# Float16 for the choice of experts, the gate tiles' dots ahead of the low parts, and sixteen dots in a head's turn in place of fifteen

## The chip, the core and the metric

The kernel runs on one core of a Trainium2 chip, as one program. The engines spoken of are TensorE (PE, with PEld for its weight loads), VectorE (DVE), ScalarE (ACT), GpSimd (POOL) and SyncE (SP, which only starts transfers here). Each follows its own list of instructions in order, and they meet through semaphores. The metric is the time of one execution on the device in microseconds. Lower is better.

## The reference

The program computes two transformer blocks one after the other, for 512 tokens of width 1024. The change lies wholly in the second half of the first block, `peer_ffn`, a feed-forward layer that picks its experts by product keys:

```
q = (xi @ w_q).reshape(n, PEER_HEADS, 2, PEER_KEY_DIM)          # 8 heads
s = jnp.einsum('nhpc,hpkc->nhpk', q, sub_keys)                  # 128 keys a side
ts, ti = lax.top_k(s, PEER_TOPK)                                # 16 a side
cand_s = ts[:, :, 0, :, None] + ts[:, :, 1, None, :]            # 16 x 16 sums
cand_i = ti[:, :, 0, :, None] * PEER_NKEYS + ti[:, :, 1, None, :]
best_s, best_p = lax.top_k(cand_s, PEER_TOPK)
idx = jnp.take_along_axis(cand_i, best_p, axis=-1)              # 16 experts a head
gate = jax.nn.softmax(best_s, axis=-1)
act = jax.nn.gelu(jnp.einsum('nd,nhkd->nhk', xi, u[idx]))
return jnp.einsum('nhk,nhkd->nd', gate * act, v[idx])
```

There are 128 x 128 = 16384 experts, with a row of 1024 numbers each in `u` and in `v`.

## The kernel before

**Two ways through the experts.** For the first 384 tokens (ND) the kernel computes the products with all 16384 experts on PE: 128 slabs of `u`, 128 experts each, give activations that are stored in DRAM ("early"), and later a gate matrix, zero where an expert was not picked, multiplies them before the slabs of `v` are applied. For the last 128 tokens (one to a partition) it does what the reference does: it fetches the 8 x 16 = 128 picked rows of `u` for each token and takes their dot products with the token. Pick k is a column of 128 row numbers in `own_at`. POOL fetches it with one indirect transfer of 128 rows (512 KB), L2435 in `own_fetch`, and DVE takes the dot product in `own_dots` at L2123, one custom instruction for each pick. There are 8 row buffers for the picks of the head stage and 4 for those of the gate tiles, and a fetch waits until its buffer's last dot is done (semaphore `own_dotted`). A dot waits for its row (`own_in`).

**The head stage.** Eight turns, one a head. PE's part of turn h: two query slabs, the scores of both sides (L1078), and ten slabs of `u` woven in (`woven`), 12 slabs in all. Each slab passes as three float16 products, so its float32 numbers are cut into a high part (ACT, L519, which also scales the slab in place, L521) and a low part (POOL, L532, `cut_low_scaled`). PE waits for the low part. POOL runs three slabs ahead of PE: its loop of turn h starts with the low part of the fourth slab of head h (woven slab number 1, counted from 0), and each of its 12 steps j is one low part and then the fetches of that step.

**Which picks POOL fetches when.** In the turns 1 to 6 POOL's loop spreads TURN_PICKS = 15 fetches over the 12 steps: turn h fetches the picks (h-1)*15 to (h-1)*15+14. A head has 16 picks, and the first pick of each head waits on POOL for `head_done`, that is for DVE's last instruction of that head's choice (L2110). The first fetch of a turn has such a wait as well. So the pick that waits stands at step 1 in turn 2, at step 2 in turn 3, at step 3 in turns 4 and 5 and at step 4 in turn 6; the fetches ahead of it are picks of a head before. Turn 7 fetches four more picks in its last steps.

**DVE's turn.** DVE starts turn h when the scores of head h are copied out of PSUM (`s_out`), and then runs `choose`. It is in three parts with a third of the dots ahead of or between them (`own(0)`, `own(1)`, `own(2)`): first the dots 0 to 4 of the turn, then the top 16 of each side (L2058 to L2063), then the dots 5 to 9, then the candidates (L2068), the top 16 of them (L2071 to L2079, with `gsub_out` given at L2076), then the dots 10 to 14, then the experts' numbers: for each side a comparison of `posf` with 0 to 15 into `sel` (L2089), a product of `sel` with `tif` (L2094) and a sum over it (L2105), and the softmax of the gates. The last instruction is L2110, which gives `head_done`. Turns 0 and 7 have no dots. ACT's turn h+1 begins with the exponential of head h's gates (L1588), which waits for L2076; only behind it in ACT's order stand the copies of the queries (L1578) and of the scores (L1584) of head h+1.

**Between the stages.** After turn 7 PE does four more slabs, then waits for `head_done` of the last head and transposes the experts' numbers and gates (L1125). ACT copies them out (L1631), DVE casts them (from L2146 on), and the gate tiles begin.

**The gate tiles.** Six tiles of 64 tokens, each in eight octets. For an octet DVE writes one-hot matrices in float16 (`one_hots`, L2159 to L2164, which gives `hot_out`), ACT writes half of the low ones (L1644, which waits for L2159), PE multiplies them into the gate matrix (L1140 and L1141, which wait for `hot_out`) and ACT copies that out (L1662). In each tile PE also does five slabs of `u`. Their high parts come from ACT (L513), their low parts from DVE (L526). DVE's order is written out in `tile_turn`: behind the octet's one-hots stand the low parts that are due (`cuts.upto`), then a dot if the octet's number is in TILE_DOTS = (0, 2, 4, 5, 6). The eight dots that are left (TAIL_PICKS) come behind the tiles.

## Time and profile before

| | |
|---|---|
| three runs | 2394.67, 2402.81, 2405.39 us |
| median | 2402.81 us |
| the profiled execution | 2406.6 us, of which the span of the trace is 2404.9 us |
| granted TensorE clock over the span | 0.988 |
| head stage, from the first query slab to the wait for the last head | 405.6 to 852.9 us |
| gate tiles | 874.5 to about 1065 us |
| value slabs, and the second block | about 1098 us to the end |

The profile was read in this order: the page (busy shares and the chain that ended last), the view of waits for the head stage, the busy time of the engines turn by turn, the time line of POOL and DVE at the start of a turn, and the same for one gate tile. Times in the time line count from the start of the span. A wait's releaser is the instruction that set the semaphore last.

### The profile page before, as it was taken

The numbers are of one execution on the slowest core, as the hardware profiler recorded it, in microseconds if no ns is written. First come the engines' busy times: TensorE is split into PE (matmuls) and PEld (weight loads), VectorE is DVE, ScalarE is ACT, GpSimd is POOL, SyncE is SP. The second block draws the span as 40 slices with busy tenths as digits, with TensorE's granted clock in tenths as the row PEclk, the third lists the DMA queues.
The fourth block names the chain that finished last, engine by engine and source line by source line (L and its number), as shares of the span: only waits on it lengthen the run. The fifth ranks groups of instructions, "written<-read, shape, count | busy, mean of one in ns | idle before, by whom it ended". The sixth has DMA issues, their size and how long they took to land.

```text
span 2404.9 us, 38222 instructions
## 1 busy us (share of the span) xinstructions
PE 2324.7 (97%) x13522; PEld 1292.8 (54%) x13522; DVE 1698.6 (71%) x2994; ACT 1104.9 (46%) x1677; POOL 553.1 (23%) x418
## 2 busy tenths in 40 slices
PE   7999999999999989999999999999999999999998
PEld 4446764555555556665555555564444444444454
DVE  5327765588899979977988888878453447776235
ACT  4266443665666668864333333343522233333133
POOL 0001001667788631123322222204000010000001
PEclk9999999999999999999999999999999999999989
DMA  5200022587889659989999999933232323233321
GB/s 180 79 27 1 1 71 88 185 275 281 309 313 332 225 172 345 343 322 359 381 364 361 362 361 357 362 126 114 88 114 97 104 89 105 96 102 108 102 74 53
DMA packets 164871, 470.67 MB, mean 196 GB/s; under 512 B 17744, under 2 KB 70736, under 8 KB 163984
## 3 DMA queue, kind: packets, MB, share of 16 engines
q1 hardware_dynamic: 109312, 289.48, 34.8%
q0 software_dynamic: 36864, 134.23, 15.1%
q10 hardware_dynamic: 18576, 45.36, 5.0%
q8 instruction: 76, 1.25, 0.2%
q14 instruction: 43, 0.35, 0.0%
HBM read 421.56 MB, written 47.45 MB: 195 GB/s over the span
## 4 chain that ended last, share of the span: by engine, by line
PE 74%; DVE 16%; ACT 2%; issue 2%; POOL 2%; DMA 2%; DVEq 2%; SPq 0%; ACTq 0%
PE psum L552 22%; PE psum L553 22%; PE psum L554 22%; DVE arena L2123 4%; DVEq L2048 2%; DMA arena<-in_urows,arena 2%; POOL arena L532 1%; PE psum L434 1%; POOL arena L2435 1%; PE psum L1140 1%; PE psum L1017 1%; PE psum L1141 1%; PE psum L895 1%; DVE arena L526 1%; DVE arena L1919 1%
## 5 line engine op out<-in xcount | busy, mean ns | idle before, releaser
L552 PE MATMUL psum<-arena 128*128 128x384 f16 (+2 forms) x3648 | 1262.4, 347 | 18.9 <-DVE arena L483 7.6
L553 PE MATMUL psum<-arena 128*128 128x384 f16 (+2 forms) x3648 | 1265.5, 347 | 0.0
L554 PE MATMUL psum<-arena 128*128 128x384 f16 (+2 forms) x3648 | 1258.6, 347 | 0.0
L552 PEld LDWEIGHTS psum<-arena 128*128 128x128 f16 x3648 | 355.0, 97 | 353.1 <-issue 37.8
L554 PEld LDWEIGHTS psum<-arena 128*128 128x128 f16 x3648 | 354.0, 97 | 324.0 <-issue 6.7
L553 PEld LDWEIGHTS psum<-arena 128*128 128x128 f16 x3648 | 354.1, 97 | 311.2 <-issue 7.1
L526 DVE SCALAR_TENSOR_TENSOR arena<-arena 128x1024 f16<-128x1024 f32 x216 | 265.5, 1233 | 287.4 <-ACT arena L513 286.1
L513 ACT ACTIVATE arena<-arena 128x1024 f16<-128x1024 f32 x216 | 226.3, 1051 | 237.5 <-PE psum L554 226.1
L1678 ACT ACTIVATE arena<-arena 128x1024 f16<-128x1024 f32 x128 | 135.3, 1057 | 299.7 <-PE psum L554 278.6
L532 POOL TENSOR_TENSOR arena<-arena 128x1024 f16<-128x1024 f32 x104 | 230.7, 2218 | 103.9 <-ACT arena L521 102.3
L445 POOL TENSOR_TENSOR arena<-arena 128x512 f32<-128x512 f32 x15 | 19.8, 1318 | 890.4 <-ACT arena L399 890.4
L2435 POOL DMA_INDIRECT arena<-in_v,arena x128 | 132.5, 1035 | 356.8 <-DVE arena L2134 324.4
L2435 POOL DMA_INDIRECT arena<-in_urows,arena x128 | 133.6, 1044 | 210.1 <-DVE arena L2123 153.4
L2123 DVE CUSTOM_DVE_ANT_0 arena<-arena,psum 128x1024 f32<-128x1024 f32 x128 | 151.4, 1215 | 29.7 <-DMA arena<-in_urows,arena 28.1
L2134 DVE SCALAR_TENSOR_TENSOR arena<-arena 128x1024 f32<-128x1024 f32 x126 | 161.0, 1279 | 1.7 <-DMA arena<-in_v,arena 1.7
L2211 DVE SCALAR_TENSOR_TENSOR arena<-arena 128x1024 f16<-128x1024 f32 x128 | 156.0, 1219 | 0.0
L1604 ACT ACTIVATE arena<-psum 128x384 f32<-128x384 f32 x128 | 62.2, 486 | 133.6 <-PE psum L554 130.8
L2205 DVE TENSOR_TENSOR arena<-arena 128x384 f16<-128x384 f32 x128 | 71.4, 558 | 61.8 <-ACT arena L1683 61.4
L519 ACT ACTIVATE arena<-arena 128x1024 f16<-128x1024 f32 x104 | 109.0, 1048 | 11.0 <-DMA arena<-in_w 10.9
L521 ACT ACTIVATE arena<-arena 128x1024 f32<-128x1024 f32 x104 | 109.9, 1057 | 3.3
L1785 ACT ACTIVATE arena<-psum 128x512 f32<-128x512 f32 x44 | 26.3, 598 | 143.6 <-PE psum L554 143.6
L399 ACT ACTIVATE arena<-arena 128x512 f32<-128x512 f32 (+1 forms) x48 | 29.7, 630 | 86.1 <-DVE arena L2030 33.4
(258 smaller groups left out, 2226.8 us busy)
## 6 DMA issues: line engine op xcount, KB each, us to landing
arena<-in_w SPq DMA_DIRECT2D x320, 512.0 KB
arena<-in_v SPq DMA_DIRECT2D x128, 512.0 KB
early_activations<-arena ACTq DMA_DIRECT2D x124, 192.0 KB
arena<-early_activations SPq DMA_DIRECT2D x124, 192.0 KB
gate_matrix<-arena ACTq DMA_DIRECT2D x5, 4096.0 KB, 16.1
arena<-gate_matrix SPq DMA_DIRECT2D x32, 640.0 KB
arena<-in_xT SPq DMA_DIRECT2D x4, 512.0 KB, 6.3
arena<-in_urows,arena POOLq DMA_INDIRECT x128
```

What stands on the lines that cost most here:

```text
L513: nc.scalar.activation(wh[:, s, :], wraw[:, s, :], ACT.Copy, scale=WS).then_inc(high_cut, 1)
L521: nc.scalar.activation(wraw[:, s, :], wraw[:, s, :], ACT.Copy, scale=WS).then_inc(high_cut, 1)
L526: nc.vector.scalar_tensor_tensor(out=wl[:, s, :], in0=wraw[:, s, :], scalar=WS, in1=wh[:, s, :], op0=ALU.mult, op1=ALU.subtract).then_inc( ...
L532: nc.gpsimd.tensor_tensor(wl[:, s, :], wraw[:, s, :], wh[:, s, :], ALU.subtract).then_inc(low_cut, 1)
L552: nc.tensor.matmul(ps, a_h, b_h, start=first, stop=False)
L553: nc.tensor.matmul(ps, a_h, b_l, start=False, stop=False)
L554: return nc.tensor.matmul(ps, a_l, b_h, start=False, stop=last)
L1678: nc.scalar.activation(vh[:, s, :], vraw[:, s, :], ACT.Copy, scale=WS).then_inc(vhigh_cut, 1)
L2123: nc.vector.tensor_tensor_reduce(out=x, in0=x, in1=own_tok, scale=1.0, scalar=0.0, op0=ALU.mult, op1=ALU.add, accum_out=own_dot[:, k:k + 1 ...
L2134: ins = nc.vector.scalar_tensor_tensor(out=to, in0=x, scalar=by, in1=to, op0=ALU.mult, op1=ALU.add)
L2211: nc.vector.scalar_tensor_tensor(out=vl[:, s, :], in0=vraw[:, s, :], scalar=WS, in1=vh[:, s, :], op0=ALU.mult, op1=ALU.subtract).then_inc( ...
L2435: nc.gpsimd.indirect_dma_start(own_row(b, k >= PICKS), None, table, bass.IndirectOffsetOnAxis(own_at[:, k % PICKS:k % PICKS + 1], 0)).then ...
```

## The change

It has four parts. The lists of instructions on PE and ACT stay as they are.

1. **Float16 in the choice.** `tif`, `posf` and `sel` become float16, in half of the words they had. A float16 copy of the numbers 0 to 15, `io16h`, is made once in turn 0. The comparison (L2089) and the product (L2094) now read and write float16. The sum (L2105) reads float16 and still writes float32. The numbers are below 128, so they stay exact.
2. **Sixteen dots in a head's turn.** TURN_PICKS goes from 15 to 16, so that the head stage holds 96 picks in place of 90. The parts of a turn have 5, 5 and 6 dots. POOL's spread of the fetches over its steps follows: one, one, two, and so on four times over.
3. **Four dots in a gate tile.** TILE_DOTS loses octet 5, so that the tiles hold 24 dots in place of 30.
4. **The tiles' dots ahead of the low parts.** In `tile_turn` the dot of an octet stands right behind its one-hots, ahead of the low parts that are due.

```
-TURN_PICKS = 15
+TURN_PICKS = 16
-TILE_DOTS = (0, 2, 4, 5, 6)
+TILE_DOTS = (0, 2, 4, 6)
...
-        tif = v3(r.take(2 * TT * TOP), 2)
+        tif = v3(r.take(2 * TT * TOP)[:, 0:TT * TOP].bitcast(f16), 2)
...
-        posf = v3(r.take(2 * TT * TOP), 2)
-        sel = v3(r.take(2 * TT * 256), 2)
+        posf_words = r.take(2 * TT * TOP)
+        posf = v3(posf_words[:, 0:TT * TOP].bitcast(f16), 2)
+        io16h = posf_words[:, TT * TOP:TT * TOP + TOP // 2].bitcast(f16)
+        sel = v3(r.take(2 * TT * 256)[:, 0:TT * 256].bitcast(f16), 2)
...
                         sel4(side), tiles(posf[:, side, :]).unsqueeze(3).to_broadcast(full),
-                        io16.unsqueeze(1).unsqueeze(1).to_broadcast(full), ALU.is_equal)
+                        io16h.unsqueeze(1).unsqueeze(1).to_broadcast(full), ALU.is_equal)
...
-                third = TURN_PICKS // 3
+                at_part = [part * TURN_PICKS // 3 for part in range(4)]
                 dve.wait_ge(s_out, 2 * h + 2)
+                if h == 0:
+                    nc.vector.tensor_copy(io16h, io16)
...
                     one_hots(t * OCT + i)
+                    if i in TILE_DOTS:
+                        own_dots(picks + TILE_DOTS.index(i), 1)
                     if t == 0 and i == 1:
                         dve.wait_ge(low_cut, cuts.n)
                     if i:
                         cuts.upto(N_U + e + (i - 1 + (i - 1) // 4 + ((i - 1) % 4 == 3)) // 2 + 3)
                     elif t:
                         cuts.upto(N_U + e - 1 + 3)
-                    if i in TILE_DOTS:
-                        own_dots(picks + TILE_DOTS.index(i), 1)
```

How this moves instructions is shown at two places. The rows are those of the programs' lists; what stands in brackets are the semaphores that an instruction waits for. Nearly everything lies in one tensor, `arena`, so a transfer of rows is told by `in_urows`.

The first place is POOL at the start of turn 3: the last two steps of turn 2 and the steps that follow. The low part of a slab is the TENSOR_TENSOR, a fetch is the DMA. Before:

```order
L532 TENSOR_TENSOR arena<-arena 128x1024 [waits high_cut]
L2435 DMA arena<-in_urows,arena 128x1024 [waits own_dotted] x2
L532 TENSOR_TENSOR arena<-arena 128x1024 [waits high_cut]
L2435 DMA arena<-in_urows,arena 128x1024 [waits own_dotted,head_done]
L532 TENSOR_TENSOR arena<-arena 128x1024 [waits high_cut]
L2435 DMA arena<-in_urows,arena 128x1024 [waits own_dotted]
L532 TENSOR_TENSOR arena<-arena 128x1024 [waits high_cut]
L2435 DMA arena<-in_urows,arena 128x1024 [waits own_dotted,head_done]
L532 TENSOR_TENSOR arena<-arena 128x1024 [waits high_cut]
L2435 DMA arena<-in_urows,arena 128x1024 [waits own_dotted] x2
```

In the changed program (L534 is the low part there, L2440 the fetch):

```order
L534 TENSOR_TENSOR arena<-arena 128x1024 [waits high_cut]
L2440 DMA arena<-in_urows,arena 128x1024 [waits own_dotted] x2
L534 TENSOR_TENSOR arena<-arena 128x1024 [waits high_cut]
L2440 DMA arena<-in_urows,arena 128x1024 [waits own_dotted,head_done]
L534 TENSOR_TENSOR arena<-arena 128x1024 [waits high_cut]
L2440 DMA arena<-in_urows,arena 128x1024 [waits own_dotted]
L534 TENSOR_TENSOR arena<-arena 128x1024 [waits high_cut]
L2440 DMA arena<-in_urows,arena 128x1024 [waits own_dotted] x2
L534 TENSOR_TENSOR arena<-arena 128x1024 [waits high_cut]
```

The wait for `head_done` that names the head just chosen stood in front of the third fetch of the turn (the one in front of the first asks for a head that was done long before). Now it stands in front of the first fetch, and there is no second one in the turn. The low part that stood between them, and the two fetches, are behind the wait now. The doubled fetch has moved up to the third step.

The second place is DVE in a gate tile, from the last one-hots of octet 4 to the first of octet 6. L526 is a low part of a slab, the two L2123 are one dot. Before:

```order
L2164 TENSOR_TENSOR arena<-arena 128x512
L526 SCALAR_TENSOR_TENSOR arena<-arena 128x1024 [waits high_cut]
L2123 ISA arena<-arena,psum 128x1024 [waits own_in1,own_turned]
L2123 ISA arena 128x1
L2159 TENSOR_TENSOR arena<-arena 128x1024 [waits g_done]
L2160 TENSOR_TENSOR arena<-arena 128x1024
L2162 TENSOR_TENSOR arena<-arena 128x1024 [waits hot_slab_out]
L2164 TENSOR_TENSOR arena<-arena 128x512
L2123 ISA arena<-arena,psum 128x1024 [waits own_in2,own_turned]
L2123 ISA arena 128x1
L2159 TENSOR_TENSOR arena<-arena 128x1024 [waits g_done]
```

In the changed program (L2169 ends an octet, L2125 is the dot, L528 the low part, L2164 begins an octet):

```order
L2169 TENSOR_TENSOR arena<-arena 128x512
L2125 ISA arena<-arena,psum 128x1024 [waits own_in2,own_turned]
L2125 ISA arena 128x1
L528 SCALAR_TENSOR_TENSOR arena<-arena 128x1024 [waits high_cut]
L2164 TENSOR_TENSOR arena<-arena 128x1024 [waits g_done]
L2165 TENSOR_TENSOR arena<-arena 128x1024
L2167 TENSOR_TENSOR arena<-arena 128x1024 [waits hot_slab_out]
L2169 TENSOR_TENSOR arena<-arena 128x512
L2164 TENSOR_TENSOR arena<-arena 128x1024 [waits g_done]
```

The dot of octet 4 has moved in front of the low part, and the dot of octet 5 is gone.

## Rows read from the trace of the kernel before

**Rows 1.** The page: busy time, share of the span and instructions of each engine.
```profile
PE 2324.7 (97%) x13522; PEld 1292.8 (54%) x13522; DVE 1698.6 (71%) x2994; ACT 1104.9 (46%) x1677; POOL 553.1 (23%) x418
```

**Rows 2.** Waits from 405 to 853 us: who waited for whom; us in total, times, longest.
```profile
POOL arena L2435 <- DVE arena L2110: 36.0, 6, 10.4
ACT arena L1588 <- DVE arena L2076: 30.3, 5, 8.7
DVE arena L2140 <- ACT arena L1584: 26.1, 2, 14.3
DVE arena L2123 <- DMA arena<-in_urows,arena: 24.2, 15, 3.5
...
PE psum L552 <- POOL arena L532: 4.5, 4, 2.2
PE psum L1125 <- DVE arena L2110: 4.5, 1, 4.5
```

**Rows 3.** Busy time of the engines in DVE's turns 2, 2 to 6, 6, 7.
```profile
core 0: us, PE busy (x) PEld busy (x) DVE busy (x) ACT busy (x) POOL busy (x), PEclk, DMA share, GB/s
532.70:594.00 61.30, 57.62 (x332) 32.65 (x331) 48.92 (x145) 36.77 (x45) 43.97 (x29) 0.97 0.79 284
532.70:814.10 281.40, 272.34 (x1592) 156.13 (x1591) 254.36 (x720) 176.29 (x215) 217.44 (x139) 0.99 0.84 295
758.40:814.10 55.70, 54.24 (x323) 31.31 (x321) 54.41 (x143) 35.08 (x44) 40.98 (x24) 1.00 0.76 262
814.20:852.60 38.40, 34.24 (x211) 20.10 (x209) 37.22 (x114) 24.76 (x30) 26.91 (x13) 0.98 0.72 234
```

**Rows 4.** DVE's waits for rows: turn 2 (532.7 to 594.0 us), then turn 4 (651.5 to 704.7).
```profile
DVE arena L2123 <- DMA arena<-in_urows,arena: 10.8, 5, 3.5
...
DVE arena L2123 <- DMA arena<-in_urows,arena: 1.7, 2, 1.2
```

**Rows 5.** Time line of POOL at the start of turn 3: start us, us, line, what; idle before it.
```profile
594.40 0.95 POOL L2435 DMA_INDIRECT arena<-in_urows,arena  x1 [9.04 <-DVE arena L2110]
...
597.69 0.95 POOL L2435 DMA_INDIRECT arena<-in_urows,arena  x1 [0.16 <-issue]
598.94 0.94 POOL L2435 DMA_INDIRECT arena<-in_urows,arena  x1 [0.30 <-issue]
```

**Rows 6.** Time line of DVE at the start of turn 3: the first four dots.
```profile
594.11 1.21 DVE L2123 CUSTOM_DVE_ANT_0 arena<-arena,psum 128x1024 f32<-128x1024 f32 x1
...
595.25 1.22 DVE L2123 CUSTOM_DVE_ANT_0 arena<-arena,psum 128x1024 f32<-128x1024 f32 x1
...
598.79 1.22 DVE L2123 CUSTOM_DVE_ANT_0 arena<-arena,psum 128x1024 f32<-128x1024 f32 x1 [2.33 <-DMA arena<-in_urows,arena]
...
603.56 1.22 DVE L2123 CUSTOM_DVE_ANT_0 arena<-arena,psum 128x1024 f32<-128x1024 f32 x1 [3.53 <-DMA arena<-in_urows,arena]
```

**Rows 7.** Time line of ACT around PE's wait in turn 4: activations of three woven slabs.
```profile
650.06 0.49 ACT L1604 ACTIVATE arena<-psum 128x384 f32<-128x384 f32 x1 [1.38 <-PE psum L554]
...
653.97 0.49 ACT L1604 ACTIVATE arena<-psum 128x384 f32<-128x384 f32 x1 [1.38 <-PE psum L554]
...
661.88 0.49 ACT L1604 ACTIVATE arena<-psum 128x384 f32<-128x384 f32 x1 [5.39 <-PE psum L554]
```

**Rows 8.** DVE's float32 and float16 products of two tensors: ns min/median/max over the program.
```profile
L2094 DVE TENSOR_TENSOR arena<-arena x16: 1219/1227/3166, 452.6 to 845.0; 128x1024 f32<-128x1024 f32 x16
L2089 DVE TENSOR_TENSOR arena<-arena x16: 1218/1226/3168, 450.2 to 840.8; 128x1024 f32<-128x1024 f32 x16
L2159 DVE TENSOR_TENSOR arena<-arena x48: 681/685/2519, 859.0 to 1051.5; 128x1024 f16<-128x1024 f16 x48
```

**Rows 9.** PE's waits in the gate tiles, 874 to 1062 us, then one tile's busy times.
```profile
PE psum L1140 <- DVE arena L2164: 10.2, 18, 1.1
...
920.90:951.30 30.40, 28.22 (x248) 18.99 (x248) 28.63 (x48) 25.87 (x59) 5.73 (x5) 1.00 0.92 345
```

**Rows 10.** Time line of DVE in a gate tile: the low part behind octet 4.
```profile
950.12 1.23 DVE L526 SCALAR_TENSOR_TENSOR arena<-arena 128x1024 f16<-128x1024 f32 x1 [1.62 <-ACT arena L513]
```

More of the change, by code:

```diff
@@ L2137, in _ @@
             for h in range(PH):
-                third = TURN_PICKS // 3
+                at_part = [part * TURN_PICKS // 3 for part in range(4)]
                 dve.wait_ge(s_out, 2 * h + 2)
+                if h == 0:
+                    nc.vector.tensor_copy(io16h, io16)
                 nc.vector.tensor_copy(gsum[:, 12 + h % 2:13 + h % 2], s_[h % 2][:, 0, 0:1])
-                choose(h, s_[h % 2], lambda part: own_dots((h - 1) * TURN_PICKS + part * third, third)
+                choose(h, s_[h % 2], lambda part: own_dots((h - 1) * TURN_PICKS + at_part[part],
+                                                           at_part[part + 1] - at_part[part])
                        if 0 < h < PH - 1 else None)
```

## The prediction

> **What bounds the kernel now.** The page comes first: PE is busy 97% of the span [rows 1], so only what makes PE stand or slows its clock can be won. The windows of the stages show two places with such gaps that the change touches, the head stage and the gate tiles. In the head stage the view of waits says who sets the pace [rows 2]. ACT waits 30.3 us in 5 turns for L2076 of the head before, and ACT is what hands PE its next scores. POOL waits 36.0 us for `head_done` (L2110) and so PE 4.5 us for low parts, and PE waits 4.5 us more for the last head. DVE waits for rows (24.2 us) and, only at the starts of turns 0 and 1, for scores (26.1 us in two waits). So from turn 1 on DVE's chain sets the end of the stage: five turns, 2 to 6, take 281.4 us, and turn 7, without dots, 38.4 [rows 3]. The start of turn 3 shows why early turns are longer (turn 2: 61.3 us, turn 6: 55.7 [rows 3]). DVE's first dot starts at 594.11 and the second 1.14 us later, with rows fetched ahead [rows 6]. POOL stood 9.04 us for L2110 and issues the next fetch at 594.40 [rows 5], some 0.35 us behind `head_done`. Its dot can start at 598.79, 4.4 us later; the next fetch, at 597.69, has its dot at 603.56, 5.9 us later [rows 6]. Two fetches with a low part between them stand 3.3 us apart, two in a row 1.25 [rows 5]. Row waits are 10.8 us in turn 2, where one row was fetched ahead, 1.7 in turn 4, where three were [rows 4], and none in turn 6 with five. **What spares DVE the waits is the picks of an older head at the start of a turn.**
>
> **Float16.** A float32 product L2094 takes 1.227 us, a float16 one with its inner numbers side by side 0.685 [rows 8]. Both inputs of L2094 run over 16 neighbours, so I take 0.685: 2 x 0.54 = 1.09 us a turn. The comparison L2089 has the same 1.226 us [rows 8], but one of its inputs is a single number read 16 times. Its bounds are 1.226 and 0.685, and I take the first, the row of the same pattern; the other would give 1.09 us a turn more. The float16 sum L2105 has no row: between nothing and 0.5 us each; I take nothing. For the casts I count no gain either. The copy `io16h` lies in turn 0, ahead of a wait of 11.8 us (26.1 less the longest, 14.3 [rows 2]), and costs nothing.
> The Trainium skill (Vector Engine (DVE) Microarchitecture Reference, 5.1 Performance modes) says that a two-source operation on 2-byte numbers whose input is one element read 16 times ran at the plain rate, and at the doubled rate where a row is read again. By that rule the comparison gains nothing and the product does, as taken above; no row of this trace shows it.
>
> **Sixteen dots a turn.** A dot occupies DVE for 1.14 us, so with float16 the work of a turn stays: +1.14 - 1.09. But 16 is the number of picks of a head. Turn h now fetches exactly the picks of the head just chosen, and POOL meets its wait in front of the first fetch in every turn 2 to 6. DVE asks for five of these rows at once. From `head_done` the fetches start at +0.35, +3.6, +6.9, +8.2 and +11.4 us (steps of 3.3, 3.3, 1.25 and 3.3 [rows 5]; the second to fourth low parts are ready, since ACT is up to four slabs ahead while PE stands). With 4.4 us for the first and 5.9 for the others [rows 5, 6] the dots start at 4.7, 9.5, 12.8, 14.1 and 17.3 and end at 18.5, where five dots need 5.7. That is 12.8 us of waits, 2.0 more than turn 2 has now [rows 4]. The dots of the second part come after the top 16 of both sides; their rows are then there. Bounds: rows that land the moment they are issued leave 7.9 us (POOL's pace alone); a second step of 1.5 us in landing, as from 4.4 to 5.9, for the last one gives 14.3.
> A turn is then 61.3 + 2.0 + 1.14 - 1.09 = 63.35 us. I start from turn 2 and not from turn 6, because DVE is busy 48.9 us in the one and 54.4 in the other [rows 3] with the same instructions: products and casts of DVE wait where POOL is at a low part (L2089 up to 3.168 us in place of 1.226 [rows 8]), and in turn 2 POOL stands, as it will.
> The Trainium skill (SBUF — State Buffer, SBUF: two separate sides) has it that the port pair of these two engines is held by one of them for a whole instruction; the trace agrees, with 1.94 us of surplus on L2089.
>
> **Who is last at the end of the stage.** In turn 1 the doubled fetch moves up a step, which brings one of its rows some 2 to 3.3 us sooner; of that I take 1.5 us (between 0 and 3.3). So turn 2 starts at 531.2 and turn 6 at 531.2 + 4 x 63.35 = 784.6. PE is now held at woven slab 2 in each turn, as POOL's low part for it stands behind the wait: it goes on 3.5 us after `head_done` (0.35 + 0.95 + 2.2). A woven slab takes 3.91 us (650.06 to 653.97 [rows 7]); where PE stood for 2.2 us [rows 2] the next activation came 7.91 us later [rows 7], so about 1.8 us went on a lower clock (0.97 granted in turn 2, that is stretches at 1.2 in place of 2.4 GHz [rows 3]). For a stand of 7 us I take 3. From there to the end of the stage PE has 22 woven slabs (86.0), two query slabs of 512 columns (2 x 3.91 x 512/384 = 10.4) and the scores (2): 98.4. PE arrives at 784.6 + 3.5 + 3 + 98.4 = 889.5. DVE ends turn 7 at 784.6 + 63.35 + 38.4 - 1.1 = 885.3. PE is last, and the transposes start at 889.5 in place of 852.9: **+36.6 us**. The wait of 4.5 us there [rows 2] goes, and is inside this sum. PE does not hold DVE in the turns: the next scores are copied out at 3.5 + 3 + 31.3 + 10.4 + 7 = 55 us of a turn of 63.
>
> **The gate tiles.** PE waits 10.2 us for one-hots, in 18 waits, three a tile [rows 9]. Before octet 5 DVE waits 1.62 us for ACT with the low part, with a dot behind it [rows 10]. The dot now lies in that hole (1.14 us), and the dot of octet 5 is gone (1.14 more for octets 6 and 7). Each of the three waits is at most 1.1, so all go: **-10.2 us**, at most 6 x (30.4 - 28.2) = 13 by PE's busy time in a tile [rows 9], and nothing if ACT, busy 25.9 of 30.4, becomes late instead. The low parts come 1.14 us later, but DVE makes them three slabs (over 10 us) ahead. The picks 120 to 127 stay behind the tiles as they were, and the value slabs and the second block have the same instructions.
>
> **Sum.** 36.6 - 10.2 = +26 us. On the profiled execution's 2406.6 us that is 2433; it lies 3.8 above the median of 2402.8, so I forecast 2402.8 + 26 = **2429 us**.
>
> **Rivals.**
> *Cheap rows (no change).* While POOL stands, no weights are loaded either, so rows may land at once. Then a turn waits 7.9 us, not 12.8; with comparisons at 0.685 too it is 57.4 us, turn 6 starts at 760.8, PE arrives at 865.7: +12.8 - 10.2, so 2405. For it: the transfers are the busiest resource beside PE (0.84 [rows 3]). Against it: the first row, fetched after 9 us of standing, still took 4.4 us.
> *PE sets the turn (faster).* If the rows cost under 4 us a turn, DVE falls back on `s_out`, and row waits hide behind it as in turn 1. The turn is then PE's: 3.5 + 31.3 + 10.4 + 7 = 52.2 without loss of clock. Turn 6 starts at 740.0, PE arrives at 841.9: -11 - 10.2, so 2382. It decides from row waits of about 3 us a turn downwards; the break-even is at 6. Against it stand POOL's steps of 3.3 us, which alone make 7.9.
> *PE late as well (slower still).* Loaded queues (7.4 us a row) and a longer stretch at 1.2 GHz behind each stand give turns of 66: +47, and with no gain in the tiles (ACT late) 2440 to 2450.
> *Float16 brings nothing* (L2094 stays at 1.23): 1.09 x 4 = +4 us, inside the forecast's own range.
>
> **How the numbers follow.** The forecast's mechanism, with turns of 61.5 to 65 us and 8 to 13 us won in the tiles, gives 2419 to 2439 and has 0.68. Cheap rows 0.12, PE sets the turn 0.06, PE late too 0.14. About 0.5% (12 us) is what a measurement of this kernel tells from no change. So slower by more than that 0.82, within it 0.12, faster 0.06. The range of 8 in 10 runs from 2407, at the edge of the cheap rows, to 2446.
>
> **What would show it.** Right: POOL waits for L2110's successor about 13 us in each turn 2 to 6, in front of the first fetch; five turns of 61 to 65 us; the first dot of each 4 to 5 us behind `head_done`; row waits of over 60 us in all; PE standing 6 us or more at woven slab 2; L2094 at 0.69 and L2089 at 1.23 us; no wait for `head_done` at the transposes; PE's waits for one-hots under 2 us. Wrong: turns below 58 us, or gate tiles as long as before.

## The result, and the profile after

The changed kernel takes 2425.11 us (median of seven runs) against 2403.07 us for the kernel before on the same chip (median of seven). One of the seven, 3022.67 us at a granted clock of 0.749, is a slow run that the ratio leaves out; the other six have a median of 2423.69. The ratio is 1.0092, with a 95% interval from 1.0068 to 1.0117: **slower by 22 us** (20.6 by the medians without that run), where 26 were forecast. The profiled execution took 2427.66 us, its span 2425.9 us (2404.9 before), so the spans differ by 21.0 us.

The page's busy line, beside [rows 1], shows DVE busy 26 us less and TensorE's work as before:

```profile
PE 2331.6 (96%) x13522; PEld 1299.2 (54%) x13522; DVE 1672.3 (69%) x2995; ACT 1104.1 (46%) x1677; POOL 552.4 (23%) x418
```

The view of waits from 408 to 885 us (who waited for whom: us in total, times, longest), beside [rows 2]:

```profile
ACT arena L1606 <- PE psum L556: 143.5, 77, 11.5
...
POOL arena L2440 <- DVE arena L2112: 70.1, 6, 14.1
DVE arena L2125 <- DMA arena<-in_urows,arena: 66.8, 24, 4.8
...
PE psum L554 <- POOL arena L534: 33.3, 5, 7.5
...
ACT arena L1590 <- DVE arena L2078: 11.3, 2, 8.0
```

POOL's wait for `head_done` has doubled (36.0 to 70.1 us), DVE's for rows has nearly tripled (24.2 to 66.8), and PE now stands 33.3 us for low parts where it stood 4.5. ACT's wait for L2078 (L2076 before), which had been the sign that DVE's chain sets the pace, has shrunk from 30.3 to 11.3 us: ACT now stands in front of its activations (L1606, 143.5 us), behind a late PE, and so comes late to L1590 itself. Two chains are held by the same wait, DVE's by its rows and PE's by its low parts.

The windows of turns 2 to 6, turn 2, turn 6, turn 7 and of the stretch from the transposes to the first octet, beside [rows 3] (columns as there):

```profile
535.40:847.10 311.70, 277.21 (x1577) 157.51 (x1578) 238.02 (x732) 174.56 (x212) 220.79 (x145) 0.93 0.78 276
535.40:596.20 60.80, 53.44 (x304) 30.41 (x304) 46.63 (x148) 35.28 (x43) 41.90 (x28) 0.94 0.78 278
779.20:847.10 67.90, 62.09 (x361) 35.67 (x362) 52.09 (x147) 37.67 (x46) 53.24 (x33) 0.95 0.80 280
847.20:879.70 32.50, 32.50 (x202) 19.28 (x201) 30.95 (x115) 23.84 (x29) 22.11 (x12) 1.00 0.76 243
884.70:903.70 19.00, 17.13 (x110) 10.52 (x109) 13.76 (x15) 13.33 (x21) 11.76 (x6) 1.00 0.54 176
```

Turns 2 to 6 take 311.7 us in place of 281.4. The turns start at 535.4, 596.3, 657.4, 718.3, 779.1 and 847.2: four of 60.8 to 61.2 us and one, turn 6, of 68.

The start of turn 2 shows how. First POOL's time line (start us, us, engine, line, what; in brackets the idle time before it and who ended it), then DVE's:

```profile
535.76 0.95 POOL L2440 DMA_INDIRECT arena<-in_urows,arena  x1 [13.76 <-DVE arena L2112]
536.73 2.15 POOL L534 TENSOR_TENSOR arena<-arena 128x1024 f16<-128x1024 f32 x1
539.03 0.95 POOL L2440 DMA_INDIRECT arena<-in_urows,arena  x1 [0.16 <-issue]
...
542.31 0.95 POOL L2440 DMA_INDIRECT arena<-in_urows,arena  x1 [0.16 <-issue]
543.57 0.94 POOL L2440 DMA_INDIRECT arena<-in_urows,arena  x1 [0.30 <-issue]
...
546.85 0.96 POOL L2440 DMA_INDIRECT arena<-in_urows,arena  x1 [0.16 <-issue]
```
```profile
540.11 1.22 DVE L2125 CUSTOM_DVE_ANT_0 arena<-arena,psum 128x1024 f32<-128x1024 f32 x1 [4.56 <-DMA arena<-in_urows,arena]
...
543.98 1.22 DVE L2125 CUSTOM_DVE_ANT_0 arena<-arena,psum 128x1024 f32<-128x1024 f32 x1 [2.64 <-DMA arena<-in_urows,arena]
...
548.01 1.22 DVE L2125 CUSTOM_DVE_ANT_0 arena<-arena,psum 128x1024 f32<-128x1024 f32 x1 [2.80 <-DMA arena<-in_urows,arena]
...
549.26 1.22 DVE L2125 CUSTOM_DVE_ANT_0 arena<-arena,psum 128x1024 f32<-128x1024 f32 x1
...
553.19 1.22 DVE L2125 CUSTOM_DVE_ANT_0 arena<-arena,psum 128x1024 f32<-128x1024 f32 x1 [2.70 <-DMA arena<-in_urows,arena]
```

`head_done` comes at 535.5, the end of L2112. The five fetches start on POOL 0.3, 3.5, 6.8, 8.1 and 11.4 us behind it, one low part of 2.15 us between most of them, and the dots start 4.35, 4.95, 5.70, 5.69 and 6.34 us behind their fetches (the fourth dot follows the third without a row wait, so its row may have been there sooner). Of the 18.9 us from `head_done` to the end of the fifth dot, 12.7 are waits. Over a whole turn DVE stands 12.8 to 14.3 us in front of dots, in each of the turns 2 to 6.

PE at the same moment (matmuls of 384 columns):

```profile
539.02 0.48 PE L554 MATMUL psum<-arena 128*128 128x384 f16 x1 [4.70 <-POOL arena L534]
539.29 0.53 PE L555 MATMUL psum<-arena 128*128 128x384 f16 x1
...
543.13 0.39 PE L555 MATMUL psum<-arena 128*128 128x384 f16 x1
```

PE has stood 4.70 us for the low part that POOL began at 536.73. It comes back with matmuls of 0.53 us that start 0.32 us apart, and keeps that pace until 543.1; then they take 0.33 us again and start 0.16 us apart. The granted clock is 0.50 from 539.0 to 543.1 and 0.99 from there to 550. These are the two levels of its clock, 1.2 and 2.4 GHz; turns 2 to 6 show a mean granted clock of 0.93 in place of 0.99 [rows 3]. The stands of the five turns are 4.7, 7.4, 7.5, 7.0 and 6.7 us.

In the gate tiles, the waits of PE from 903 to 1082 us and then one tile, beside [rows 9]:

```profile
PE psum L1142 <- ACT arena L1646: 1.9, 1, 1.9
```
```profile
932.50:961.30 28.80, 27.95 (x250) 19.23 (x249) 27.57 (x46) 25.70 (x60) 5.46 (x5) 1.00 0.91 345
```

No wait of PE for one-hots is left. A tile takes 28.8 us, not 30.4.

**Where the 21.0 us come from**, in the two profiled executions:

| stretch | before, us | after, us | difference |
|---|---|---|---|
| start of turn 1 | 478.7 | 481.4 | +2.7 |
| from there to the transposes | 374.2 | 403.3 | +29.0 |
| transposes to the first octet | 21.6 | 19.0 | -2.5 |
| first to last octet | 180.1 | 170.1 | -10.0 |
| last octet to the end | 1350.2 | 1352.1 | +1.9 |

The first line and the last, +4.6 us together, are not taken as the change's. The instructions there are the same but for turn 0, which has one copy more and the float16 and ends in a wait for scores of 11.8 us in both traces. The runs below show both shifts with other kernels too (turn 1 starts anywhere from 477.1 to 481.6 us, and the last line reads 1350.6 to 1352.2 in them). The three lines between sum to +16.5.

### The profile page after: what moved, and what is told of

It reads as the page before. It is cut to its first block, busy times and chain, and to the rows that moved or that the text cites. A ratio compares the mean times of both kernels' runs of the same rounds, so it can differ in the third digit from the quotient of the medians.

```text
span 2425.9 us, 38197 instructions
## 1 busy us (share of the span) xinstructions
PE 2331.6 (96%) x13522; PEld 1299.2 (54%) x13522; DVE 1672.3 (69%) x2995; ACT 1104.1 (46%) x1677; POOL 552.4 (23%) x418
## 4 chain that ended last, share of the span: by engine, by line
PE 78%; DVE 11%; POOL 3%; DMA 2%; ACT 2%; issue 2%; DVEq 1%; SPq 0%; ACTq 0%
PE psum L554 23%; PE psum L556 23%; PE psum L555 23%; DVE arena L2125 3%; POOL arena L534 2%; DMA arena<-in_urows,arena 2%; POOL arena L2440 1%; PE psum L1142 1%; PE psum L436 1%; PE psum L1143 1%; DVEq L2050 1%; PE psum L897 1%; PE psum L1019 1%; DVE arena L2070 1%; DVE arena L1921 1%
## 5 line engine op out<-in xcount | busy, mean ns | idle before, releaser
L554 PE MATMUL psum<-arena 128*128 128x384 f16 (+2 forms) x3648 | 1264.8, 348 | 47.8 <-POOL arena L534 33.3
L528 DVE SCALAR_TENSOR_TENSOR arena<-arena 128x1024 f16<-128x1024 f32 x216 | 265.7, 1234 | 280.3 <-ACT arena L515 279.5
L534 POOL TENSOR_TENSOR arena<-arena 128x1024 f16<-128x1024 f32 x104 | 227.3, 2185 | 92.6 <-ACT arena L523 91.2
L2440 POOL DMA_INDIRECT arena<-in_v,arena x128 | 132.4, 1035 | 356.8 <-DVE arena L2136 325.3
L2125 DVE CUSTOM_DVE_ANT_0 arena<-arena,psum 128x1024 f32<-128x1024 f32 x128 | 151.8, 1218 | 75.4 <-DMA arena<-in_urows,arena 70.3
L2440 POOL DMA_INDIRECT arena<-in_urows,arena x128 | 136.4, 1065 | 238.4 <-DVE arena L2125 141.7
L1606 ACT ACTIVATE arena<-psum 128x384 f32<-128x384 f32 x128 | 62.6, 489 | 182.8 <-PE psum L556 180.0
L401 ACT ACTIVATE arena<-arena 128x512 f32<-128x512 f32 (+1 forms) x48 | 29.8, 632 | 85.3 <-DVE arena L2032 33.3
```

What stands on the lines that cost most here:

```text
L528: nc.vector.scalar_tensor_tensor(out=wl[:, s, :], in0=wraw[:, s, :], scalar=WS, in1=wh[:, s, :], op0=ALU.mult, op1=ALU.subtract).then_inc( ...
L534: nc.gpsimd.tensor_tensor(wl[:, s, :], wraw[:, s, :], wh[:, s, :], ALU.subtract).then_inc(low_cut, 1)
L554: nc.tensor.matmul(ps, a_h, b_h, start=first, stop=False)
L2125: nc.vector.tensor_tensor_reduce(out=x, in0=x, in1=own_tok, scale=1.0, scalar=0.0, op0=ALU.mult, op1=ALU.add, accum_out=own_dot[:, k:k + 1 ...
L2440: nc.gpsimd.indirect_dma_start(own_row(b, k >= PICKS), None, table, bass.IndirectOffsetOnAxis(own_at[:, k % PICKS:k % PICKS + 1], 0)).then ...
```

## The experiments

The theory tested is the forecast's: **the rows of a turn's first part belong to the head just chosen, so they are fetched behind `head_done`, and DVE waits for them.** It stands against the sixteenth dot by itself (R stands for rows in some expectations, W for a cheap wait), and against **the hold** (H): that it is POOL's standing in front of PE's low part, with PE's slow clock behind it, that costs. Ratios are to the kernel before on the same chip, with their 95% intervals; times are medians. The runs lie on three chips, so a difference in us is worked out from the ratios, times the 2401 us of the kernel before.

### Sixteen dots a turn and four a tile, alone

Of the change only this, with float32 in the choice and the dots behind the low parts (`at_part` stands in place of `third`, as in the change, since 16 has no whole third).

```
-TURN_PICKS = 15
+TURN_PICKS = 16
-TILE_DOTS = (0, 2, 4, 5, 6)
+TILE_DOTS = (0, 2, 4, 6)
```

> The kernel before with sixteen dots a turn and four a gate tile, and nothing else. Theory R (rows): the loss is the fetch that now waits for the head just chosen, so this alone shows it whole: DVE waits about 13 us for rows in each of the turns 2 to 6, turns of 62 us (61 of the changed kernel plus 1.09 of float32 products), the transposes some 33 us later than before; in the tiles one dot less in octet 5 gives back about 1.14 us of the 1.7 a tile, so +25 us in all, 2428. Rival W (work): the sixteenth dot itself, 1.14 us on an engine that sets the pace, is the loss: 6 x 1.14 = +7 less 7 in the tiles, 2403, turns of 2 to 6 longer by 1.1 us each.

**2435.45 us, 1.0135 [1.011, 1.016].** Its waits in the head stage:

```profile
DVE arena L2123 <- DMA arena<-in_urows,arena: 73.1, 25, 4.7
...
PE psum L552 <- POOL arena L532: 41.8, 5, 9.9
```

The pattern of the whole change is there: turns of 61.9 to 66.0 us, 12.9 to 14.6 us of row waits in each. The loss is this part's, 32 us of it (25 were expected; two turns of 65.2 and 66.0 us are longer than the 62 said); the other parts must give some of it back. In the tiles the fifth dot's going gives 5.3 us of the 6.8 expected: first to last octet is 174.8 us in place of 180.1, and PE's waits for one-hots are 2.4 us in place of 10.2.

### All but this: float16 and the dots ahead, fifteen and five

```
-TURN_PICKS = 16
+TURN_PICKS = 15
-TILE_DOTS = (0, 2, 4, 6)
+TILE_DOTS = (0, 2, 4, 5, 6)
```

> The changed kernel with fifteen dots a turn and five a tile again: float16 and the dots ahead of the low parts stay. Theory R: row waits as in the kernel before (24 us in all), products at 0.69 us, the head stage 5 to 8 us shorter, the tiles 5 to 7 us shorter by the moved dots (1.14 of the 1.7 us a tile): 2388 to 2393. Rival (float16 or the order does harm of its own): 2403 or more.

**2388.70 us, 0.9941 [0.992, 0.9962]**, faster by 14 us. Turns 2 to 6 are 57.1, 56.1, 52.5, 53.4 and 52.0 us. Its waits for rows in the head stage:

```profile
DVE arena L2125 <- DMA arena<-in_urows,arena: 21.8, 10, 4.0
```

Between this kernel and the changed one stand only the sixteenth dot and the tile's fifth: 36 us.

### Float16 alone

The changed kernel with fifteen dots, five a tile, and the dots of the tiles behind the low parts again.

> The kernel before with float16 in the choice alone. If DVE sets the pace of the head stage: 1.09 us less in each of the turns 1 to 7, 5 to 8 us in all, 2395 to 2398, product 0.69 us, comparison 1.22. If what DVE saves only turns into longer waits for POOL's low parts (the products lose their time to the same port): no change, 2403.

**2396.02 us, 0.9973 [0.9956, 0.999]**, -6.5 us. The same kernel was run again for its trace:

> The float16 choice alone once more, for a trace in which the clock is granted as in the others: the product at 0.69 us, the comparison and the sum still at 1.2 us, and 1.1 us less busy time of DVE a turn than before; turns 2 to 6 of together 276 to 281.4 us, the gate tiles as long as before (180 us).

The operations of the choice in it (ns min/median/max, first and last start us, forms), the comparison, the product and the sum, beside [rows 8]:

```profile
L2091 DVE TENSOR_TENSOR arena<-arena x16: 1218/1226/3175, 453.0 to 826.6; 128x1024 f16<-128x1024 f16 x16
L2096 DVE TENSOR_TENSOR arena<-arena x16: 678/693/2633, 455.5 to 828.5; 128x1024 f16<-128x1024 f16 x16
L2107 DVE TENSOR_REDUCE arena<-arena x16: 1202/1211/1216, 462.3 to 833.1; 128x64 f32<-128x1024 f16 x16
```

The product went to 0.69 us, the comparison stayed at 1.22, and the sum too stays at 1.2 us with float16 at its input: two of them took 2.34 us in a turn before and take 2.34 after. Turns 2 to 6 are 271.1 us together, lower than the 276 to 281.4 expected. Single executions differ there by themselves: the next kernel doesn't touch the head stage and shows 275.7 where the kernel before had 281.4. The timed 6.5 us are the better number, though their interval runs from 2.4 to 10.6 us.

### The tiles' dots ahead of the low parts, alone

```
                     one_hots(t * OCT + i)
+                    if i in TILE_DOTS:
+                        own_dots(picks + TILE_DOTS.index(i), 1)
                     if t == 0 and i == 1:
...
-                    if i in TILE_DOTS:
-                        own_dots(picks + TILE_DOTS.index(i), 1)
```

> The kernel before with the tiles' dots ahead of the low parts, still five a tile. The dot of octet 4 fills the wait for ACT (1.14 us), so PE's waits for one-hots fall from 1.7 to 0.6 us a tile: 6 x 1.14 = 7 us less, 2396. Rival: the hole only moves, because the octet 5 dot stays and ACT hands its high part over no sooner: 0 to 2 us, 2401 to 2403.

**2394.14 us, 0.9972 [0.9955, 0.9989]**, -6.7 us. First to last octet is 171.8 us in place of 180.1, with PE's waits for one-hots down from 10.2 to 2.4 us. So the order alone wins 8.3 of the tiles' 10 us, with five dots a tile still in place. Taking the fifth away, alone, won 5.3 (above). The two overlap: either closes most of the same waits, and only both close them all.

### Three ways to free the start of a turn

If the rows of the first part are what costs, DVE must not ask for them there. If the hold is what costs, POOL must not stand in front of a low part. Three kernels separate the two. The first keeps POOL's order and moves DVE's dots to the second and third part of the turn:

```
-                at_part = [part * TURN_PICKS // 3 for part in range(4)]
+                at_part = [0, 0, TURN_PICKS // 2, TURN_PICKS]
```

> The changed kernel with the turn's dots in parts of 0, 8 and 8 in place of 5, 5 and 6: POOL's list is untouched, so POOL stands and PE is held at woven slab 2 as before, but no dot is asked for at once. Theory R (DVE's row waits are the cost): row waits under 4 us a turn, and what is late next is PE, held 3.5 us behind the choice and with 50 us of work behind it: turns of 54 to 56 us, transposes at 860, 2395 to 2400. Rival H (the hold on PE and its clock is the cost): turns stay near 61 and the time at 2425.

**2405.47 us, 1.0019 [1.0003, 1.0035]**: some 17 us of the loss are gone, but not the 25 to 30 expected.

```profile
POOL arena L2440 <- DVE arena L2112: 66.2, 6, 13.7
DVE arena L2125 <- DMA arena<-in_urows,arena: 40.1, 24, 3.5
...
PE psum L554 <- POOL arena L534: 24.8, 5, 6.5
```

POOL is held as long as in the changed kernel (66.2 us against 70.1) and PE 24.8 us, yet turns 2 to 5 are 57.9 to 58.7 us, not 61. The rows still cost 6.2 to 8.3 us a turn, since the second part now asks for eight rows in a row, and that comes sooner than POOL has fetched them.

The second leaves DVE's dots (5, 5, 6) and moves the fetches behind the fourth step, two a step, so that POOL does its low parts first and doesn't hold PE:

```
-                        for k in range((h - 1) * TURN_PICKS + j * TURN_PICKS // TURN,
-                                       (h - 1) * TURN_PICKS + (j + 1) * TURN_PICKS // TURN):
-                            if j == 0 or k % TOP == 0:
+                        for k in range((h - 1) * TURN_PICKS + max(j - 4, 0) * 2,
+                                       (h - 1) * TURN_PICKS + max(j - 3, 0) * 2):
+                            if k % TOP == 0:
```

> The changed kernel with POOL's sixteen fetches of a turn in its last eight steps, two a step, so that four more low parts stand ahead of the wait for the head just chosen: PE is not held any more, but the rows come as late as ever for the five dots at the turn's start. Theory R: row waits of 12 to 15 us a turn stay, turns of 61 to 66 us, the time at 2425 to 2440, although PE's waits for low parts (33 us in the changed kernel) go. Rival H (the hold on PE is the cost): 2395 or less.

**2430.85 us, 1.0122 [1.0101, 1.0144]**: no better than the changed kernel.

```profile
DVE arena L2125 <- DMA arena<-in_urows,arena: 75.2, 25, 13.3
ACT arena L1590 <- DVE arena L2078: 75.2, 6, 14.5
...
PE psum L1080 <- ACT arena L1580: 40.9, 6, 8.8
```

The hold is gone: PE has no wait for low parts, and POOL waits 2.9 us at most for L2112. The row waits are still there (11.3 to 12.0 us a turn, 17.8 in turn 1), turns are 59.4 to 61.4 us, and PE stands no less than in the changed kernel, only at another place: 40.9 us at its scores, which wait for ACT, which waits 75.2 us for L2078 on DVE. **So the hold isn't the cause:** without it the turns are as long, as long as DVE waits for its rows. PE stands because DVE's chain is late, and where it stands is a matter of who is asked first.

The third has both edits:

> Both at once: the fetches in the last eight steps, and the dots in parts of 0, 8 and 8. No row is asked for before it had time to land and PE is not held. Expected by theory R: row waits under 3 us a turn, turns of 52 to 54 us, set by DVE with the port waits partly back, 5 x 8 = 40 us less than the changed kernel and some less in turn 7: 2375 to 2385, faster than both kernels. If PE's rest of the turn is the bound all the same: 2395.

**2406.15 us, 1.0029 [1.0018, 1.0039]**, a miss by 20 us or more. Turn 1 takes 62.3 us, the others 55.6 to 57.7, with 3.7 to 4.6 us of row waits in each.

```profile
POOL arena L2440 <- DVE arena L2112: 29.5, 5, 6.2
...
DVE arena L2125 <- DMA arena<-in_urows,arena: 28.7, 30, 2.6
```

Two fetches and a low part take POOL 4.5 us, more than the 3.91 of a woven slab, so that PE stands for low parts in the second half of a turn, 8.3 us in 18 waits of at most 0.5. DVE's turn is work of 50 to 53 us plus the row waits and 1 us of small gaps, which is more than PE's 51.2. I hadn't counted either. Against the first of the three kernels the turns 2 to 6 are 13.0 us shorter in all (281.0 and 294.1), but turn 1 is 11.0 longer (62.3 and 51.3), for having all its fetches late, and turn 7 4.8 longer (37.6 and 32.8), so nothing is won.

### Sixteen dots with older picks first

The last pair keeps sixteen dots a turn, sixteen fetches by the same spread, and the parts of 5, 5 and 6. What changes is which picks they are: turn 1 takes ten, the turns 2 to 6 sixteen each, of which the first six are of the head before. A tile has five dots again, since 90 picks are done by turn 6.

```
-HEAD_PICKS = (PH - 2) * TURN_PICKS
-TILE_DOTS = (0, 2, 4, 6)
+TURN_LO = (0, 0, 10, 26, 42, 58, 74, 90)
+HEAD_PICKS = TURN_LO[-1]
+TILE_DOTS = (0, 2, 4, 5, 6)
...
-                at_part = [part * TURN_PICKS // 3 for part in range(4)]
+                lo, n = TURN_LO[h], TURN_LO[min(h + 1, PH - 1)] - TURN_LO[h]
+                at_part = [part * n // 3 for part in range(4)]
...
-                choose(h, s_[h % 2], lambda part: own_dots((h - 1) * TURN_PICKS + at_part[part],
+                choose(h, s_[h % 2], lambda part: own_dots(lo + at_part[part],
...
+                        lo, picks = TURN_LO[h], TURN_LO[h + 1] - TURN_LO[h]
+                        for k in range(lo + j * picks // TURN, lo + (j + 1) * picks // TURN):
```

> Sixteen dots in the turns 2 to 6 but ten in turn 1, so that each turn starts with six picks of an older head; five dots a tile again, float16 and order of the change kept. Theory R: no row waits in turns 2 to 6, POOL stands 0 to 3 us a turn, PE is not held. Two ways from there: if DVE's waits for POOL's low parts stay as small as in the changed kernel (1.5 us a turn), turns of 49 to 51 us, and PE's own 51.2 us a turn becomes the bound, 2375; if they come back as in turn 6 of the kernel before (10 us, busy 54.4), turns of 54 to 56 us, 2390 to 2395.

**2380.79 us, 0.9913 [0.9891, 0.9935]**, the fastest of all: 21 us below the kernel before and 43 below the changed one, with the same sixteen dots in each of the turns 2 to 6. It lies between the two values expected, 2375 and 2390 to 2395. The window of turns 3 to 6:

```profile
590.50:795.40 204.90, 204.90 (x1218) 118.93 (x1217) 199.12 (x587) 135.25 (x165) 164.52 (x107) 1.00 0.90 315
```

PE is busy for the whole of the window, at full clock: four turns of 51.2 us, which is PE's own time. The first dots of turn 3, on DVE, behind the last instruction of the choice:

```profile
590.43 0.16 DVE L2113 SCALAR_TENSOR_TENSOR arena<-arena 128x16 uint32<-128x16 f32 x1
...
590.58 1.21 DVE L2126 CUSTOM_DVE_ANT_0 arena<-arena,psum 128x1024 f32<-128x1024 f32 x1
...
591.71 1.21 DVE L2126 CUSTOM_DVE_ANT_0 arena<-arena,psum 128x1024 f32<-128x1024 f32 x1
```

No row is waited for; the dots follow each other by 1.14 us. POOL doesn't wait for `head_done` for a microsecond anywhere. Turn 2 is longer, 55.4 us. This kernel is rid of the row waits and of the hold at once, so it speaks against the sixteenth dot as the cause and doesn't tell those two apart; the three kernels above do.

The same picks with the float32 choice of before:

> The float32 choice, the tiles' dots ahead of the low parts with five a tile, and the lagged picks: ten in turn 1 and sixteen in each of the turns 2 to 6, of which the first six belong to the head before. It differs from the run with the order alone (2394.1 us) in the picks alone, and from the lagged run with float16 (2380.8 us) in the arithmetic alone. By my theory, that which head's picks open a turn decides, most of what the lagged run gained stays: DVE's turn is 1.1 us longer than with float16 and DVE has that to spare against PE's 51.2 us in some turns only, so turns of 51.2 to 53 us and 2381 to 2388 us. By the rival, that the float16 product was what brought DVE below PE's time a turn, turns are those of the run with the order alone (53 to 58 us) and the time is 2392 us or more.

**2389.61 us, 0.995 [0.9932, 0.9967]**. Against the order alone (0.9972, the same arithmetic) the picks bring 5.3 us; with float16 on both sides (0.9941 to 0.9913) they bring 6.7. With intervals of 4 to 5 us either way on each ratio the two can't be told apart. The result lies between the two expectations. Turns 4 and 5 show why: DVE is busy 50.8 us in each, of 52.1, and the rest are small gaps and no wait for scores, so DVE's 52.1 is just above PE's 51.2 and sets the turn; 1.1 us less with float16 puts it just below. Turn 2 has 58.3 us, with DVE busy 55.4 of them and 1.4 of row waits. And at the end of the stage PE waits 4.46 us for the last head again, as in [rows 2]; in the lagged kernel with float16 it doesn't.

## Why the forecast was right, and where its steps were not

**The mechanism** held in each of its parts. Sixteen is a head's number of picks, so POOL's wait stands in front of the first fetch of every turn: 13.7 to 14.1 us each from turn 2 on, about 13 said. The fetches' steps, said to be 0.35, 3.6, 6.9, 8.2 and 11.4 us, were 0.3, 3.5, 6.8, 8.1 and 11.4. Row waits were said to be 12.8 us a turn and were 12.8 to 14.3. That it is the rows and not the hold, the first two of the three kernels show; that it is not the sixteenth dot, the lagged one.

**The turn** was mis-sized: 63.35 us said, 60.9 measured in turns 2 to 5, and 68.0 in turn 6. The step that failed is the one that starts from turn 2 of before and its 48.9 us of DVE work, plus 1.14, less 1.09. The window of turn 2 after has 46.6 us, 2.3 less. Of these 0.5 are at the candidates (L2068 took 3.29 us in turn 2 of before, L2070 2.81 after) and 1.9 at the shift of L2084. Both are DVE instructions that take longer while POOL is at a low part. The shift in turn 2 of before (time lines of POOL and DVE, columns as above):

```profile
583.19 2.17 POOL L532 TENSOR_TENSOR arena<-arena 128x1024 f16<-128x1024 f32 x1
...
583.32 2.10 DVE L2084 TENSOR_SCALAR arena<-arena 128x64 uint32<-128x64 uint32 x1
```

After, the last stretch of turn 2 and that of turn 6 are (windows, columns as above, POOL's busy time the fifth):

```profile
580.00:596.00 16.00, 12.46 (x78) 7.62 (x75) 15.37 (x31) 12.88 (x16) 2.15 (x1) 1.00 0.37 129
830.00:847.00 17.00, 17.00 (x109) 10.51 (x108) 16.48 (x23) 13.50 (x18) 11.37 (x5) 1.00 0.67 201
```

and in the two turns the shift (L2086), and the cast, comparisons and products take:

```profile
564.39 0.23 DVE L2065 CAST arena<-arena 128x128 f16<-128x128 uint32 x1
...
588.53 0.19 DVE L2086 TENSOR_SCALAR arena<-arena 128x64 uint32<-128x64 uint32 x1
...
589.20 2.36 DVE L2091 TENSOR_TENSOR arena<-arena 128x1024 f16<-128x1024 f16 x2
591.64 1.29 DVE L2096 TENSOR_TENSOR arena<-arena 128x1024 f16<-128x1024 f16 x2
...
809.94 2.78 DVE L2065 CAST arena<-arena 128x128 f16<-128x128 uint32 x1
...
835.51 0.19 DVE L2086 TENSOR_SCALAR arena<-arena 128x64 uint32<-128x64 uint32 x1
...
836.18 4.31 DVE L2091 TENSOR_TENSOR arena<-arena 128x1024 f16<-128x1024 f16 x2
840.56 3.25 DVE L2096 TENSOR_TENSOR arena<-arena 128x1024 f16<-128x1024 f16 x2
```

The shift beside the low part took 2.10 us; 0.19 is its own time. In turn 2 after, POOL ends its last low part of the loop at 582.9 and then stands in front of `head_done` until 596.6 (2.15 us busy of 16), and in turns 3 to 5 likewise, so the end of DVE's choice runs free: 2 x 1.22 for the comparisons and 2 x 0.69 for the products. In turn 6 the loop of turn 7 follows, which has no wait in front, POOL is at low parts (11.4 us of 17), and the cast (which in turn 2 starts as a low part of POOL ends, at 564.39), the comparisons and the products take 2.55, 1.95 and 1.96 us more, 6.5 in all. The candidates take 0.9 less, so that DVE is busy 5.5 us more than in turn 2 (52.1 and 46.6); with 1.3 us more of row waits that is most of the 7 by which turn 6 is longer. I had used this cost against the short turn 6 of before, and took turn 2 as the turn in which POOL stands. But a POOL that is held longer at the start, with fewer steps left in the turn's second half, gives DVE still more. The Trainium skill (SBUF — State Buffer, SBUF: two separate sides) has it that a DVE instruction in a two-port mode and a GpSimd instruction exclude each other for a whole instruction, and so do a DVE instruction with two SBUF inputs and a GpSimd instruction that reads SBUF; the rows agree, with 1.9 us on the shift and 2.55 on the cast.

The turn that the sum started from was also a long one of its kind. The run with the tiles' order alone has the same instructions in the head stage, and its turn 2 took 58.2 us in place of 61.3, with DVE busy 47.3 us, 1.5 of the difference at L2068 (1.75 us in place of 3.29), and 1.5 us less of row waits. One trace of a turn is no base to 3 us.

**Turn 1** was to save 1.5 us by its doubled fetch moving up. It took 54.0 us, as before (53.9): the gain was nothing, the lower of the bounds.

**Who is last.** PE, as said, at 884.7 and not 889.5 (+31.8 us, or +29.0 from the start of turn 1, where +36.6 was said); DVE is done at 879.8. The 4.8 us less are +4.2 for a later turn 2 (2.7 of them are there before turn 1, 1.5 the saving that did not come), -9.7 for four turns of 60.9, and +0.7 from the start of turn 6 on, where 3.5 + 3 + 98.4 = 104.9 was said and 105.6 measured. Turn 6's 68 us on DVE cost little for that reason: PE was last anyway. I put the slow clock at 3 us a turn; as DVE sets the length of the turns 2 to 5 (in turn 2 46.6 us busy and 13.0 of row waits, of 60.8), only that of turn 6 counts.

**The handoff** from the transposes to the first octet was not in the forecast. It is 2.5 us shorter. The row of before, beside the last one of the windows of after:

```profile
852.80:874.50 21.70, 19.73 (x109) 12.28 (x110) 11.32 (x16) 13.14 (x20) 9.98 (x5) 0.88 0.34 113
```

Before, PE had stood 4.46 us for the last head and went on at a granted clock of 0.88; now it has no wait there and the clock is 1.00. The lagged kernel with float32 has the wait too and needs 20.4 us; the kernels without it need 18.9 to 19.1. So does the third of the three kernels, though it waits 3.59 us there; not every stand is followed by a lower clock. I had counted the end of the wait, but not the clock behind it.

**The gate tiles** came out at -10.0 where -10.2 was said, by the mechanism said: all waits of PE for one-hots went. The order alone gave 8.3 of it, the fifth dot's going alone 5.3.

**Float16** was said to bring 1.09 us a turn by the product alone, nothing by the comparison, the sum and the casts. It was so: 0.69, 1.22 and 1.21 us. Timed alone it brings 6.5 us (2.4 to 10.6), where 5 turns would give 5.5. The Trainium skill (Vector Engine (DVE) Microarchitecture Reference, 5.1 Performance modes) lists copies, casts and tensor_scalar and tensor_tensor operations as those with a doubled rate, and no sum along a row; the trace agrees, with 1.21 us for 1024 float16 numbers.

**The rivals.** Cheap rows (2405) fell by the rows' landing times of 4.35 to 6.34 us. PE as the bound of a turn (2382) did not occur in the changed kernel. It did in the lagged one, at 51.2 us a turn, where I had put it at 52.2, and at 2381 us. PE late as well (2440 or more) was wrong: the slow clock was there and cost 2.2 to 2.9 us a turn, near the 3 said (PE is busy 53.4 to 54.1 us in each of the turns 2 to 5, and 51.2 at full clock in the lagged kernel), but it fell into time that PE had to spare, and turns were 61 us, not 66.

**How near 22 is to 26** is in part luck. In the two traces the three stretches of the change sum to +16.5 us, 29.0 where 36.6 was said, -2.5 that was not forecast, and -10.0 as said; the shifts of +4.6 us outside it bring this to 21.0. And the trace of before has a long head stage: 374.2 us from turn 1 to the transposes, where the run with the order alone needs 367.6 with the same instructions. Set against that one, the stage costs 35.7 us.

**What stays open**: the head stage's own spread, of 6.6 us between these two executions, is not explained. The shift of 2.7 us before turn 1 goes with TensorE's clock: from 150 to 250 us the granted clock is 0.97 in the four traces whose turn 1 starts at 481.3 to 481.6 us and 1.00 in the seven that start it at 477.1 to 479.9. Why the clock fell in some and not in others is open. Both limit how closely one trace can be set against another. Whether 96 picks in the head stage with older picks first would still gain was not tried.

## What to carry to other kernels

A count that two loops share (picks fetched a turn, picks a head) sets more than an amount of work: at 15 of 16 each turn opened with rows of an older head, at 16 none did, and one more dot of 1.14 us a turn cost over 30 (32 us alone, 36 with the other parts, each time less what the tile's fifth dot gave back). Before making a stage's batch equal to the producer's, ask which items its first requests name, and lag them so that they are old; here that, with five dots a tile kept, turned +22 us into -21. And a helper engine that stands is not only late: it also stops slowing the engine beside it, so a turn's work is to be read from a turn in which it stands at the same time as it will.

## What the runs showed that was not expected

- A sum along a row gains nothing from float16 at its input (1.21 us for 1024 numbers either way), nor does a comparison in which one input is a single number read 16 times (1.22 us), while the product with 16 neighbours on both sides went from 1.227 to 0.693 us.
- An indirect fetch of 128 rows took 4.3 to 4.5 us from its start on POOL to the dot's start where it was the first after POOL's standing, and 6.3 to 7.8 us for the fifth one behind it, in the five turns: rows got slower, not cheaper, as more were asked for.
- The order of three engines' lists decided where PE stood (low parts, scores, or transposes), not how long the turn was: 33.3 us at one place, 40.9 at another, with turns 2 to 5 of 60.9 and 60.5 us.
- A stand of PE of up to 0.5 us at some slabs (8.3 us in 18 waits, the third of the three kernels) left the granted clock of the turns 2 to 6 at 1.00, where stands of some 5 us once a turn (24.8 us in 5, the first kernel) had 0.94 to 0.97 in four of the five turns.
